# Hymba-style encoder trunk on one core: in the eighth recurrent head the keys' rotary and the splitting of the stacks stand behind the forward state chain

## The reference

```
for l in range(DEPTH):
    u = rmsnorm(h, norm_g[l])
    p = u @ w_in[l]                                   # 1024 x 9216
    hq, hf_f, hf_b, hi, hgt, aq, ak, av, agt = split(p)
    o_h = hgrn2_mixer(hq, hf_f, hf_b, hi, hgt, ...)   # 8 recurrent heads, both directions
    o_a = diff_attention_mixer(aq, ak, av, agt, ...)  # 8 heads, rotary on aq and ak
    h = h + concat(o_h, o_a) @ w_out[l]
out = rmsnorm(h, final_norm_g)[:, N_META:]
```

## Time and profile before

| | |
|---|---|
| time, median of 3 runs | 1383.63 us (1383.38 to 1385.27) |
| time of the profiled execution | 1386.13 us |
| its span, from first to last instruction | 1384.3 us |
| TensorE busy | 1369.8 us, 99% of the span |
| VectorE, ScalarE, GpSimd busy | 1045.7, 837.9 and 180.8 us |
| mean granted TensorE clock | 0.998 of full speed |
| share of the chain that ended last | PE 90%, DVE 5% |

### The profile page before, as it was taken

How to read it: one execution, slowest core, us unless ns; L and a number is a source line. 1 busy time by engine, 2 the same in 40 slices (tenths; PEclk the granted TensorE clock), 3 DMA queues, 4 the chain that set the end, 5 groups by cost and what they waited for, 6 DMA issues and landing times.

```text
span 1384.3 us, 32303 instructions
## 1 busy us (share of the span) xinstructions
PE 1369.8 (99%) x13108; PEld 1291.5 (93%) x13108; DVE 1045.7 (76%) x1765; ACT 837.9 (61%) x1802; POOL 180.8 (13%) x158
## 2 busy tenths in 40 slices
PE   9999999999999999999999999999999999999998
PEld 9999999999999999999998888888888899999987
DVE  6888778888646777877667878888886478888864
ACT  7666666665434665666555667666664456666654
POOL 1111222220000000000001122222210000000100
PEclk9999999999999999999999999999999999999999
DMA  5333322332324333333233232333333233334332
GB/s 187 115 101 93 108 87 85 108 108 80 98 63 129 99 102 100 100 92 101 69 107 104 89 108 85 108 107 108 108 89 103 88 105 107 108 108 114 113 96 76
DMA packets 76340, 140.41 MB, mean 101 GB/s; under 512 B 9504, under 2 KB 39456, under 8 KB 76192
## 3 DMA queue, kind: packets, MB, share of 16 engines
q1 hardware_dynamic: 76192, 138.35, 33.1%
HBM read 112.36 MB, written 17.30 MB: 94 GB/s over the span
## 4 chain that ended last, share of the span: by engine, by line
PE 90%; DVE 5%; issue 2%; ACT 2%; DMA 1%; SPq 0%; DVEq 0%; ACTq 0%
PE proj L1932 65%; PE far L2196 5%; PE pair L2179 3%; PE pair L2181 3%; PE far L2213 2%; PE pair L2065 1%; PE far L2198 1%; PE far L2149 1%; PE far L2150 1%; PE pair L1932 1%; PE pair L2131 1%; PE far L2153 1%; DVE w_lo L1397 1%; PE pair L2138 1%; PE far L2065 1%
## 5 line engine op out<-in xcount | busy, mean ns | idle before, releaser
L1932 PE MATMUL proj<-u_hi,w_hi 128*128 128x264 f32 (+1 forms) x1960 | 478.6, 312 | 2.6 <-DVE w_lo L1397 1.5
L1932 PE MATMUL proj<-u_hi,w_lo 128*128 128x264 f32 (+1 forms) x1960 | 458.1, 302 | 0.0
L1932 PE MATMUL proj<-u_lo,w_hi 128*128 128x264 f32 (+1 forms) x1960 | 458.0, 302 | 0.0
L1932 PEld LDWEIGHTS proj<-u_hi,w_hi 128*128 128x128 f32 x1960 | 314.7, 189 | 20.1 <-DVE w_lo L1397 1.8
L1932 PEld LDWEIGHTS proj<-u_hi,w_lo 128*128 128x128 f32 x1960 | 313.9, 188 | 13.5
L1932 PEld LDWEIGHTS proj<-u_lo,w_hi 128*128 128x128 f32 x1960 | 314.0, 188 | 10.6
L1397 DVE TENSOR_TENSOR w_lo<-w_raw,w_hi 128x1024 fp32r<-128x1024 f32 x178 | 226.1, 1270 | 34.5 <-ACT w_hi L957 34.4
L1205 ACT ACTIVATE decay<-pair,neg_max 128x528 f32<-128x528 f32 (+1 forms) x144 | 100.5, 698 | 203.3 <-DVE neg_max L1786 203.2
L957 ACT ACTIVATE w_hi<-w_raw 128x1024 fp32r<-128x1024 f32 x178 | 186.8, 1050 | 48.1 <-PE proj L1932 45.0
L1786 DVE TENSOR_REDUCE neg_max<-pair 128x1 f32<-128x528 f32 (+1 forms) x144 | 101.5, 705 | 92.0 <-PE pair L2181 90.8
L897 POOL TENSOR_TENSOR mix_lo<-mixed_t,mix_hi 128x528 fp32r<-128x528 f32 (+1 forms) x32 | 49.9, 1560 | 473.6 <-ACT mix_hi L1252 473.6
(11 more groups left out here) (257 smaller groups left out, 2243.8 us busy)
## 6 DMA issues: line engine op xcount, KB each, us to landing
w_raw<-w_units SPq DMA_DIRECT2D x178, 512.0 KB, 3.5
v_scratch<-blocks SPq DMA_DIRECT2D x128, 64.0 KB, 2.0
v_rows<-v_scratch SPq DMA_DIRECT2D x32, 256.0 KB, 2.8
o_scratch<-blocks SPq DMA_DIRECT2D x104, 64.0 KB, 2.6
q_stack<-gate_f SPq DMA_DIRECT2D x32, 132.0 KB, 2.4
k_stack<-k_stack SPq DMA_DIRECT2D x32, 132.0 KB, 2.4
o_rows<-o_scratch SPq DMA_DIRECT2D x14, 256.0 KB, 3.4
ops<-o_scratch SPq DMA_DIRECT2D x12, 256.0 KB, 2.7
```

The lines of the kernel that those rows point to most:

```text
L1932: ins = pe.matmul(out, w, x[:, tile, cols_n], start=(k == 0 and p == 0), stop=(k == last_k and p == 2))
```

## The change

Only head 7 of each layer (`HG_HEADS - 1`) is touched, and only the order of instructions. No instruction is added or removed. `finish_turn` of the keys moves from step 9 to step 11, `stack_high` of the keys on ScalarE from step 10 to step 11, `stack_low` of the queries from step 10 to step 11, and SP's `stack_other`, which stands one step behind `stack_high` of the keys, from step 11 to step 12. The queries' `finish_turn` stays where it was.

```
 def stack_steps(l, c):
 
     last = 2 * query_chunks(l) - 1
-    return (TURN_KEYS, TURN_KEYS + 1) if c < HG_HEADS else (last, last + 1 + (l == LAST))
+    return (TURN_KEYS, TURN_KEYS + 2) if c < HG_HEADS else (last, last + 1 + (l == LAST))
 
 def low_steps(l, c):
 
     last = 2 * query_chunks(l) - 1
-    return (TURN_KEYS + 1, TURN_KEYS + 2) if c < HG_HEADS else (last + 1, last + 1 + (l == LAST))
+    return (TURN_KEYS + 2, TURN_KEYS + 2) if c < HG_HEADS else (last + 1, last + 1 + (l == LAST))
...
 def turns_finished(c, s):
 
+    if c == HG_HEADS - 1:
+        wait = {"aq": 1, "ak": 3}
+        return [i for what in wait for i in units_followed(c, s - wait[what]) if UNITS[i][0] == what]
     return [i for i in units_followed(c, s - 1) if UNITS[i][0] in ("aq", "ak") and split_turn(c + 1, i)]
```

## The result

The changed kernel takes 1404.22 us (1403.4 to 1405.85, 4 runs) against 1384.45 us (1383.38 to 1385.79, 4 runs) for the kernel before: ratio 1.0138, 95% interval 1.0127 to 1.015, so 19.8 us slower. The forecast was 1397.6 us, 14.0 us slower, with a range up to 1403: the measured time is 6.6 us above the forecast and 1.2 us above the range. The direction and the places came out as written; three terms of the sum were too small, and one of them, `k_low`, had no range at all.

What follows compares the result with a forecast made beforehand. TensorE, busy 99% of the span, was taken to bound the kernel. First scores later by 4.3 us (layer 0) and 7.1 us (layer 1), gains included, plus 2.6 us of clock made +14.0 us on 1383.63: 1397.6 us, range 1392 to 1403.

Steps and rivals of the forecast that it cites:

- `k_low`: VectorE's step before `w_lo`: its duration taken unchanged from before, 1.55 and 1.88 us, inside 4.14 and 4.48 us to `w_lo`'s end.
- The gain at head 7's output: TensorE's wait for the forward states at L2149 goes: 2.21 us gained in layer 0, 1.79 us in layer 1.
- The clock's part: Layer 0, behind the old wait at head 7's output: the clock's fall goes with the wait, 1.3 us gained.
- The step with the most weight, SP's order: On SP the stack DMAs fall behind the load that waits for `w_lo`; before, they went 4 to 5 us earlier.
- landing of the last `k_stack`: Second `k_stack` DMA, issued 2.2 us behind the load: 3.4 us to land, from a line between 4.6 and 2.4 us.
- clock behind each wait: TensorE at head 8's first scores: 1.3 us charged per layer, 2.6 us together, with ends of nothing and 5.2 us.
- nothing of its own: ScalarE's rounding of the keys, 339.5 to 340.8 in layer 0, runs beside the queries' rest and so costs nothing.
- the dearer case with 4.7 us: By ring order alone `k_stack` lands nearer 4.7 than 2.4 us after issue; the sum would be 2.6 us larger.
- slower still: Rival: above 1403 us, by a clock low for longer or the values' DMAs late for head 8; chance 8%.
- The load does not hold the stacks: Rival: on SP the stacks do not wait behind the load; 1385 to 1386 us, chance 6%.
- The faster rival: The whole 5.3 us gain stays, 1378.3 us, if stacks land by 342.85 and 1033.55; chance 2%.
- the 19.2 us: Upper end of the forecast's added time: 5.6 and 8.4 us at the first scores plus 5.2 us of clock.

Runs made afterwards that it cites:

- first experiment: The changed kernel with SP's four stack DMAs back in step 11, ahead of the load that waits for `w_lo`: 1386.9 us, ratio to before 1.0014.
- second experiment: The kernel before with only the four stack DMAs moved to SP's step 12, behind the load that waits for `w_lo`: 1400.88 us, ratio 1.0109.
- fourth experiment: The changed kernel with ScalarE's `mix_hi` of head 6 ahead of the keys' rounding in head 7: 1402.42 us.
- third experiment: The changed kernel, where SP still waits for `w_lo` first but issues the stacks ahead of the load itself: 1399.6 us, ratio 1.0101.
- the last two experiments: The kernel before, queries' `stack_low` behind the forward chain and `k_stack` DMAs ahead of `q_stack`: 1382.46 us; the same with `mix_hi` ahead of the keys' rounding: 1382.03 us.

## Why the prediction was right in its places and too low in its size

**The gain at head 7's output: right.** Forecast 2.21 and 1.79 us. Measured from the start of L2141 to that of the output it is 4.59 - 2.37 = 2.22 us in layer 0 and 4.17 - 2.37 = 1.80 us in layer 1, and the forward chain starts 0.04 us behind the end of L2141, where 0.05 had been assumed. The clock's part came too: TensorE was free for the scores at 352.10 - 9.61 = 342.49, which with the 0.36 us by which the changed kernel is ahead at L2141 is the 342.85 of the forecast.

**The step with the most weight, SP's order: right.** Experiments one and two show it from both sides: with the stacks ahead of the load 17.3 us of the loss are gone, and the move of the DMAs alone costs 15 us.

**The step that failed: the sizes of three terms, `k_low` first.** In the profiled executions the span grew by 19.8 us, from 1384.3 to 1404.1, 5.8 us more than the 14.0 of the sum. Up to L2141 of layer 0 the changed kernel was 0.36 us ahead. The first scores come 6.1 us later there (352.10 + 0.36 - 346.36) against 4.3 forecast, and in layer 1 9.3 us later (1052.81 - 1035.34, less the 8.15 by which L2141 is already late) against 7.1. What follows each restart costs 2.4 and 2.3 us, against 1.3 each. These two are what is left over; half clock for about 5.3 and 4.4 us of work would be 2.7 and 2.2 us, so the clock accounts for them. Sum: -0.36 + 6.1 + 2.4 + 9.3 + 2.3 = 19.8.

| term of the sum | forecast | measured | short by |
|---|---|---|---|
| `k_low` (start to end, layers 0 and 1) | 1.55 and 1.88 us | 2.61 and 2.54 us | 1.7 us |
| landing of the last `k_stack` | 3.4 us each | 4.0 and 5.0 us | 2.2 us |
| clock behind each wait | 1.3 us each | 2.4 and 2.3 us | 2.1 us |

These 6.0 us, less the 0.36 us at the start, leave 5.7 of the 5.8. The mechanism of the loss was right, the sizes were off, all three on the same side:

- *`k_low`.* I took its duration from before, although the change delays the keys' rounding on ScalarE, and with it `mix_hi` behind it and GpSimd's `mix_lo`, which thus falls beside `k_low`. The fourth experiment shows this: without the collision it is 1.43 and 1.44 us instead of 2.61 and 2.54. The step that found the keys' rounding to cost "nothing of its own" looked at ScalarE only and not at who is started by what stands behind. The sign stood in the rows of before: the same two instructions take 1.55 us in the earlier trace rows and 1.88 us in the earlier trace rows, and in layer 1 `mix_lo` ran from 1030.55 to 1031.81, past the start of `k_low` at 1031.23.
- *The landing.* I drew a line between 4.6 us and 2.4 us. The third experiment shows that the load's bytes are the cause. The Trainium skill's rule of ring order (DMA: Bandwidth & Descriptors, "Queues, rings and completion order"), which I had given as the dearer case with 4.7 us, is nearer for layer 1. Why layer 1 takes 1 us more than layer 0 stays open; the second experiment shows the same order, 3.8 against 4.4 us. The 5.0 us is also above the 4.7 that I had as the far end.
- *The clock.* I took the cost from a stretch of 3 us at half clock behind a gap of 2.3 us. Behind 9.6 and 11.0 us it stayed at half for about 5.3 and 4.4 us of work. My own far end, twice 1.3 us for each, held it.

What broke the range is `k_low`. The far ends of the landing (9.4 us for both layers) and of the clock (5.2 us) were both in the 19.2 us, and the measured 9.0 and 4.7 us lie inside them; the 1.7 us of `k_low` had no end of its own. The kernel of the fourth experiment, which differs from the changed one in that collision alone, measured 1402.42 us, inside the range.

**One more slip, in the baseline.** I took off 1.3 us for the clock's fall in layer 0, read from a profiled execution of 1386.13 us, and then added the sum to a median of 1383.63. The 21 timed runs of the kernel before in the later session fall into two groups: seven from 1383.59 to 1384.64, all at a mean clock of 0.999, and fourteen from 1385.21 to 1386.21, all but one at 0.998. The groups suggest that in a third of the executions there was little to regain; no profile here shows such an execution. Sum and base did not belong together: with 1386.13 as its base the sum gives 1400.1 us, so the slip made the forecast lower and the miss larger. The last 0.8 of the 6.6 us is the base as well: the four runs of the kernel before that go with the result have their median at 1384.45, not 1383.63.

**The rivals.** The number of "slower still", above 1403 us, is what came, and it had been given 8%. Of its two reasons one bears a part: the clock stayed low for longer than one stretch as in the earlier trace rows, 2.1 of the 5.8 us. The other did not come: TensorE's waits in the changed kernel name none for the values' DMAs. The larger part, `k_low` and the landing, stood in no rival. "The load does not hold the stacks" gave 1385 to 1386 us, and the first experiment, which is just that kernel, measured 1386.9. The faster rival would have needed the stacks before 342.85; the only kernels that came near it changed SP's order for the keys.

## What to carry to other kernels

When a step is moved, read what else stands in that step's queue on every engine: here four DMAs of 0.6 us each moved by one step and fell behind a load that waits for another engine, and that cost 15 to 17 us, three times the 5.3 us that the reordering could have gained at best. If a wait can be shortened on the compute engine, look next at which of the transfers behind it is ready first, and issue that one first: this is what turned a loss into 2.6 to 3 us of gain. A duration copied from the old trace holds only if its neighbours on the other engines stay the same.

## What the runs showed of the hardware

**A VectorE product of two SBUF operands and GpSimd's `mix_lo` exclude each other, by turns.** A product that started while `mix_lo` ran ended only after it: 1.88 us instead of 0.70. When the VectorE instruction had started first, GpSimd's took 1.79 us instead of 1.3 and VectorE's none more. VectorE instructions with a PSUM operand ran beside it at their usual 1.11 us for three. The Trainium skill (SBUF — State Buffer, "SBUF: two separate sides") calls the port pair that both share an exclusive lock, which the one that starts first holds for its whole instruction; these rows agree.

**The clock's fall is not a function of the gap alone.** In the kernel before it did not fall behind 1.95 us without work, in the second experiment it did behind 2.02 us (0.64 from 1036.6 to 1041.4), both times at head 7's output in layer 1. In the profiled execution of the first experiment the clock fell 1 us after the restart in layer 0, to a mean of 0.55, and in layer 1 stayed at 0.51 for more than 6 us; its ten runs spread from 1385.7 to 1390.3 us, at mean clocks of 0.999 down to 0.996:

```profile
345.60:349.40 3.80, 3.80 (x21) 3.80 (x21) 2.34 (x3) 1.74 (x3) 0.00 (x0) 0.55 0.63 203
1036.10:1042.30 6.20, 6.19 (x17) 5.05 (x18) 3.46 (x4) 1.74 (x3) 0.00 (x0) 0.51 0.42 130
```

The two kernels without a wait above 0.9 us here (the last two experiments) kept their clock at 1.00 in the profiled stretches; their nine and eleven runs spread over 1.2 and 1.1 us only, where the first experiment's ten spread over 4.6.
